# Score products of 64 partitions issued for two heads in turn in both mixers, and four head buffers in the second

## The reference, cut to what matters

```
z = q @ k.T / sqrt(64)                      # per head, over the causal prefix
log_not_b = where(causal, log_sigmoid(-z), 0)
stick = reverse_cumsum(log_not_b) - log_not_b
a = where(causal, exp(log_sigmoid(z) + stick), 0)
out = a @ v

# retention, per head (width 128, rotary applied to q and k)
inner = (q @ k.T * decay) @ v
```

## Time and profile before

| | |
|---|---|
| median of 3 runs | 2847.84 us (2845.98 to 2852.53) |
| profiled execution | 2845.72 us, its span 2843.9 us |
| TensorE busy | 2767.0 us, 97% of the span |
| VectorE busy | 2099.9 us, 74% |
| ScalarE busy | 1414.8 us, 50% |
| GpSimd busy | 195.7 us, 7% |
| data read | 527.48 MB, 188 GB/s over the span |

### The profile page before, as it was taken

The page is one execution under the profiler, slowest core; times in us unless marked ns, Lnnn a source line. Parts: engine busy times, 40 slices in busy tenths (PEclk is TensorE's granted clock), DMA queues, the critical chain, the costliest instruction groups (busy, mean ns, idle before and its releaser), DMA issues.

```text
span 2843.9 us, 40048 instructions
## 1 busy us (share of the span) xinstructions
PE 2767.0 (97%) x16458; PEld 2357.3 (83%) x16458; DVE 2099.9 (74%) x3106; ACT 1414.8 (50%) x1646; POOL 195.7 (7%) x172
## 2 busy tenths in 40 slices
PE   8989999999999999999999999999999999999998
PEld 7768888788888788888888888887888888888887
DVE  7877867665553679999879955536699999799655
ACT  4454445554456555554443344484555544443443
POOL 0200002010013001210000000030011200000000
PEclk9999999999999999999999999999999999999999
DMA  8857854555553355554445555633445544455554
GB/s 331 310 182 269 320 185 173 196 178 191 192 199 134 119 179 185 187 189 164 164 166 191 177 193 192 228 125 134 171 168 190 192 165 170 157 193 176 188 195 143
DMA packets 75637, 537.41 MB, mean 189 GB/s; under 512 B 8512, under 2 KB 8896, under 8 KB 12096
## 3 DMA queue, kind: packets, MB, share of 16 engines
q1 hardware_dynamic: 75456, 534.86, 53.9%
HBM read 527.48 MB, written 7.34 MB: 188 GB/s over the span
## 4 chain that ended last, share of the span: by engine, by line
PE 65%; issue 22%; DVE 7%; ACT 4%; DMA 2%; POOL 0%; SPq 0%; DVEq 0%; POOLq 0%; ACTq 0%
PE banks L442 18%; PE banks L450 9%; PE banks L516 7%; PE banks L519 7%; PE banks L527 7%; DVE wlo L1480 3%; PE banks L490 2%; ACT whi L999 2%; PE banks L492 2%; PE banks L501 2%; PE banks L464 2%; PE banks L466 2%; PE banks L474 1%; DMA raw<-in_wkv 1%; PE banks L944 1%
## 5 line engine op out<-in xcount | busy, mean ns | idle before, releaser
L999 ACT ACTIVATE whi<-raw 128x2048 fp32r<-128x2048 f32 x438 | 838.9, 1916 | 972.5 <-issue 813.8
L1480 DVE TENSOR_TENSOR wlo<-raw,whi 128x2048 fp32r<-128x2048 f32 x438 | 1006.8, 2299 | 312.5 <-ACT whi L999 297.3
L442 PE MATMUL banks<-ht,whi 128*128 128x512 f32 x2880 | 704.8, 394 | 8.5 <-DVE big L1554 2.8
L442 PEld LDWEIGHTS banks<-ht,whi 128*128 128x128 f32 x2880 | 527.6, 189 | 113.2 <-issue 6.6
L516 PE MATMUL banks<-whi,ht 128*128 128x512 f32 x1152 | 458.1, 398 | 13.5 <-DVE ht L1544 9.0
L519 PE MATMUL banks<-whi,ht 128*128 128x512 f32 x1152 | 452.7, 393 | 0.0
L450 PEld LDWEIGHTS banks<-ht,wlo 128*128 128x128 f32 x2880 | 369.1, 191 | 14.6
L450 PE MATMUL banks<-ht,wlo 128*128 128x256 f32 x2880 | 373.4, 282 | 0.0
L527 PE MATMUL banks<-wlo,ht 128*128 128x512 f32 x1152 | 290.6, 390 | 0.0
L516 PEld LDWEIGHTS banks<-whi,ht 128*128 128x128 f32 x1152 | 217.7, 189 | 58.9 <-issue 14.6
L519 PEld LDWEIGHTS banks<-whi,ht 128*128 128x128 f32 x1152 | 217.7, 189 | 43.2
(11 more groups left out here) (274 smaller groups left out, 3425.0 us busy)
## 6 DMA issues: line engine op xcount, KB each, us to landing
raw<-in_pu SPq DMA_DIRECT2D x128, 1024.0 KB, 4.9
raw<-in_pv SPq DMA_DIRECT2D x128, 1024.0 KB, 4.9
raw<-in_win SPq DMA_DIRECT2D x52, 1024.0 KB, 5.0
big<-in_wmod SPq DMA_DIRECT2D x24, 1024.0 KB, 6.6
raw<-in_wmod SPq DMA_DIRECT2D x24, 1024.0 KB, 5.0
raw<-in_wgate SPq DMA_DIRECT2D x22, 1024.0 KB, 4.9
raw<-in_wup SPq DMA_DIRECT2D x22, 1024.0 KB, 5.2
raw<-in_wdown SPq DMA_DIRECT2D x22, 1024.0 KB, 4.9
```

Of the source, the lines that this page charges most:

```text
L442: m = e.matmul(bank[b + n], h[:, q, c[n]], M.both[:, q * 512:(q + 1) * 512], start=q == 0, stop=False, skip_group_check=True)
L999: e.activation(whi(j), slot[u][0], ACT.Copy).then_inc(*hi.mark(j))
L1480: e.tensor_tensor(wlo(j), slot[u][0], whi(j).bitcast(F32), ALU.subtract).then_inc(*lo.mark(j))
```

## The change

In the first mixer the one-head scores of steps 0 to 7 are issued two heads at a time in steps 0, 2, 4 and 6. In the second mixer the logits of two heads are issued in turn behind units 2, 4, 6 and 8, the two heads' `sticks` behind units 3, 5, 7 and 9, and the values behind units 5, 7, 9 and 10. ScalarE, VectorE and GpSimd follow that order, the ring has four buffers, and GpSimd's rotary steps 0 and 2 stand behind the logits' masks of steps 6 and 8, while 1 and 3 stand ahead of the exponentials' masks of steps 7 and 9. Retention's scores are issued for two heads in turn.

```diff
--- before.py
+++ after.py
@@ -661,7 +661,8 @@
 
             def step(i):
                 if i < 8:
-                    scores(0, (i,))
+                    if i % 2 == 0:
+                        scores(0, (i, i + 1))
                 elif i < 12:
                     scores(2, (2 * (i - 8), 2 * (i - 8) + 1))
                 if l == 0 and i == 13:
@@ -739,19 +740,23 @@
                 on.wait_ge(*normal.at((*name, "diag")))
                 e.matmul(bank[b][:, 0:256], ONES, DG[0], start=True, stop=True).then_inc(*turned.mark(("rows", l)))
 
-            def logits(h):
-                b = clear(("sb", l, h), 2 + h % 2)
-                on.wait_ge(*took_v.at(("f", l, 2 * (h // 4) + 1)))
-                p0, c = 64 * (h % 2), h // 2
+            def logits(c):
+                for h in (2 * c, 2 * c + 1):
+                    clear(("sb", l, h), 2 + h % 2)
+                on.wait_ge(*took_v.at(("f", l, 2 * (c // 2) + 1)))
                 for i in range(3):
-                    q = AG[p0:p0 + 64, SBQ + c * 256 + (i > 0) * 128:][:, 0:128]
-                    k = AG[p0:p0 + 64, SBK + c * 256 + (i > 1) * 128:][:, 0:128]
-                    m = e.matmul(bank[b][:, i * 128:(i + 1) * 128], k, q, start=i == 0, stop=True, skip_group_check=True)
-                m.then_inc(*scored.mark(("sb", l, h)))
+                    for h in (2 * c, 2 * c + 1):
+                        p0 = 64 * (h % 2)
+                        q = AG[p0:p0 + 64, SBQ + c * 256 + (i > 0) * 128:][:, 0:128]
+                        k = AG[p0:p0 + 64, SBK + c * 256 + (i > 1) * 128:][:, 0:128]
+                        m = e.matmul(bank[2 + h % 2][:, i * 128:(i + 1) * 128], k, q, start=i == 0, stop=True,
+                                     skip_group_check=True)
+                        if i == 2:
+                            m.then_inc(*scored.mark(("sb", l, h)))
 
             def sticks(h):
                 b = 2 + h % 2
-                s = ag(RING + (h % 3) * 768 + 384, 384)
+                s = ag(RING + (h % 4) * 768 + 384, 384)
                 tneg, oneg = ag(TN, 128), ag(TN + 128, 128)
                 on.wait_ge(*p_keep.at(("soft", l, h)))
                 on.wait_ge(*d_k2.at(l))
@@ -768,25 +773,28 @@
                     clear(("ov", l, 1), 1)
                 on.wait_ge(*p_keep.at(("exp", l, h)))
                 on.wait_ge(*took_a.at(("sv", l, 1)))
-                w = ag(RING + (h % 3) * 768, 384)
+                w = ag(RING + (h % 4) * 768, 384)
                 o = slice(h * 64, h * 64 + 64)
                 v = [ag(SBV + t * 512 + h * 64, 64) for t in range(2)]
                 e.matmul(bank[0][:, o], w[:, 0:128], v[0], start=True, stop=True)
                 e.matmul(bank[1][:, o], w[:, 128:256], v[0], start=True, stop=False)
                 e.matmul(bank[1][:, o], w[:, 256:384], v[1], start=False, stop=True).then_inc(*valued.mark(("sb", l, h)))
 
-            def retention_scores(h):
-                b = clear(("ret", l, h))
+            def retention_scores(c):
+                of = [bank[clear(("ret", l, 2 * c + j))] for j in range(2)]
                 on.wait_ge(*p_mul.at(("r", l, 3)))
-                p0, c = 64 * (h % 2), h // 2
-                q = [AG[p0:p0 + 64, RQ + c * 512 + i * 256:][:, 0:256] for i in range(2)]
-                k = [AG[p0:p0 + 64, RK + c * 512 + i * 256:][:, 0:256] for i in range(2)]
+                q, k = ([[AG[64 * j:64 * j + 64, x + c * 512 + i * 256:][:, 0:256] for i in range(2)] for j in range(2)]
+                        for x in (RQ, RK))
                 for i in range(2):
-                    e.matmul(bank[b][:, 0:256], k[i][:, 0:128], q[i], start=i == 0, stop=i == 1, skip_group_check=True)
+                    for j in range(2):
+                        e.matmul(of[j][:, 0:256], k[j][i][:, 0:128], q[j][i], start=i == 0, stop=i == 1,
+                                 skip_group_check=True)
                 for i in range(2):
-                    m = e.matmul(bank[b][:, 256:384], k[i][:, 128:256], q[i][:, 128:256], start=i == 0, stop=i == 1,
-                                 skip_group_check=True)
-                m.then_inc(*scored.mark(("ret", l, h)))
+                    for j in range(2):
+                        m = e.matmul(of[j][:, 256:384], k[j][i][:, 128:256], q[j][i][:, 128:256], start=i == 0,
+                                     stop=i == 1, skip_group_check=True)
+                        if i == 1:
+                            m.then_inc(*scored.mark(("ret", l, 2 * c + j)))
 
             def retention_values(h):
                 if h == 0:
@@ -814,21 +822,19 @@
                     b_unit([("rv", l, t) for t in range(2)], HT, i - 10, ready)
                 else:
                     b_unit([("rg", l, t) for t in range(2)], HT, i - 12, ready)
-                if 5 <= i < 12:
-                    for h in {5: (0, 1)}.get(i, (i - 4,)):
-                        stick_values(h)
-                if 3 <= i < 11:
+                for h in {5: (0, 1), 7: (2, 3), 9: (4, 5), 10: (6, 7)}.get(i, ()):
+                    stick_values(h)
+                if i in (3, 5, 7, 9):
                     sticks(i - 3)
-                if 2 <= i < 10:
-                    logits(i - 2)
+                    sticks(i - 2)
+                if i in (2, 4, 6, 8):
+                    logits(i // 2 - 1)
                 if i == 11:
                     retention_scores(0)
-                    retention_scores(1)
                 if i == 12:
                     retention_values(0)
                     retention_values(1)
-                    retention_scores(2)
-                    retention_scores(3)
+                    retention_scores(1)
                 if i == 13:
                     retention_values(2)
                     retention_values(3)
@@ -1244,10 +1250,10 @@
 
             def logits(h):
                 key = ("sb", l, h)
-                w = ag(RING + (h % 3) * 768, 384)
+                w = ag(RING + (h % 4) * 768, 384)
                 on.wait_ge(*scored.at(key))
-                if h >= 3:
-                    on.wait_ge(*valued.at(("sb", l, h - 3)))
+                if h >= 4:
+                    on.wait_ge(*valued.at(("sb", l, h - 4)))
                 since()
                 e.activation(w, psum(key)[:, 0:384], ACT.Abs).then_inc(*a_soft.mark((*key, 0)))
                 on.wait_ge(*a_soft.at((*key, 0)))
@@ -1258,7 +1264,7 @@
             def sticks(h):
                 key = ("sb", l, h)
                 on.wait_ge(*scored.at(("stick", l, h)))
-                e.activation(ag(RING + (h % 3) * 768, 384), psum(key)[:, 0:384], ACT.Exp).then_inc(*took_a.mark(key))
+                e.activation(ag(RING + (h % 4) * 768, 384), psum(key)[:, 0:384], ACT.Exp).then_inc(*took_a.mark(key))
 
             os = [ag(OO2 + t * 1024, 1024) for t in range(2)]
             sqs = [XN2[:, 512:1024], XN2[:, 1024:1536]]
@@ -1283,10 +1289,12 @@
                         on.wait_ge(*inv.at(name))
                         e.activation(ag(to + t * 512, 512), psum(key)[:, :], func, scale=RMS[:, t:t + 1]).then_inc(
                             *took_a.mark(key))
-                if 3 <= i < 11:
+                if i in (3, 5, 7, 9):
                     sticks(i - 3)
-                if 2 <= i < 10:
+                    sticks(i - 2)
+                if i in (2, 4, 6, 8):
                     logits(i - 2)
+                    logits(i - 1)
                 if i == 11:
                     for t in range(2):
                         key = ("ov", l, t)
@@ -1848,13 +1856,12 @@
                 if 1 <= i < 4:
                     for j in (0, 1) if i == 1 else (i,):
                         first(j)
-                if 2 <= i < 10:
-                    h = i - 2
+                for h in (i - 2, i - 1) if i in (2, 4, 6, 8) else ():
                     key = ("sb", l, h)
-                    w = ag(RING + (h % 3) * 768, 768)
+                    w = ag(RING + (h % 4) * 768, 768)
                     on.wait_ge(*a_soft.at((*key, 2)))
-                    if h >= 3:
-                        on.wait_ge(*valued.at(("sb", l, h - 3)))
+                    if h >= 4:
+                        on.wait_ge(*valued.at(("sb", l, h - 4)))
                     since()
                     e.scalar_tensor_tensor(w[:, 384:768], psum(key)[:, 0:384], 0.0, w[:, 0:384], ALU.max,
                                            ALU.add).then_inc(*took_v.mark(key))
@@ -2353,16 +2360,16 @@
                 e.tensor_tensor(pair(table), pair(table), ROWS, ALU.mult).then_inc(*p_mul.mark(("tables", l)))
             on.wait_ge(*p_mul.at(("tables", l)))
             for i in range(14):
-                if 6 <= i < 10:
+                if i in (7, 9):
                     rotary(i - 6)
-                if 3 <= i < 11:
-                    h = i - 3
+                for h in (i - 3, i - 2) if i in (3, 5, 7, 9) else ():
                     on.wait_ge(*took_a.at(("sb", l, h)))
-                    keep(ag(RING + (h % 3) * 768, 384), ("exp", l, h))
```

(8 more changed lines are left out.)

## The result

The changed kernel takes 2875.93 us (median, 2872.14 to 2876.68), the kernel before 2847.90 us in the same rounds: 1.0093 times as long, 95% interval 1.0076 to 1.0111. It is slower, as forecast, but by 28.0 us instead of 15.2, and above the upper end of the range (2869 us).

What follows compares the result with a forecast made beforehand. TensorE's own pace was taken to bound the kernel nearly everywhere. Second mixers +6.8 (waits less savings) and +9.6 (slow clock), first mixers +0.6 and -1.8, made +15.2 us: median 2863 us, range 2850 to 2869 us.

Steps and rivals of the forecast that it cites:

- side-by-side products: TensorE's scores, logits and retention for two heads in turn: savings of 5.5, 6.9 and 3.9 us, 16.3 us together.
- The third rival: Logits: side-by-side work fails, a pair costs 1.72 us, time 2865 us; chance 0.06.
- (a): Second mixer, step 3: TensorE waits 2.7 us for head 1's sticks, where before it waited for nothing.
- (b): Second mixer, step 5: TensorE waits 4.5 us at head 0's values for ScalarE's scaled `sv`, 3.2 more than before.
- (c): Second mixer, steps 7 and 9: TensorE waits about 0.3 us each for the second head's sticks.
- the drain of 1.38 us a load: ScalarE, by the skill page, behind each table load; it would make this part's waits each 2.8 us longer.
- (d): Second mixer, step 10: TensorE waits 2.3 us for heads 6 and 7's masks, behind GpSimd's rotary steps.
- the clock: Second mixers: TensorE's clock falls behind waits over 2 us, some 1.6 us each, 9.6 us in all.
- First mixers: Paired scores: layer 0 loses 0.6 us, slow clock behind step 8's wait included; layer 1 gains 1.8 us.
- The clock holds: Rival: the waits come as counted but TensorE's clock doesn't fall, +4.0 us, 2852 us; chance 0.15.
- the logits fail: Rival: two heads' logits don't run side by side, a pair costs 1.72 us, 2865 us; chance 0.06.
- The pairing pays: Rival, second mixer steps 3 to 10: ScalarE's block for a pair is short, 11.9 us saved, 2836 us; chance 0.09.

Runs made afterwards that it cites:

- e8: The changed kernel with the logits' matmuls made head after head, three and three, instead of in turn: 2876.14 us, 1.0085 times the kernel before.
- e4: e1 with ScalarE working a pair off as Abs, Abs, Exp, Exp, Ln, Ln: 2839.68 us, 0.9964 times the kernel before.
- e5: The changed kernel with ScalarE's order Abs, Abs, Exp, Exp, Ln, Ln, GpSimd's masks not moved: 2852.89 us, 1.0002 times the kernel before.
- e7: The changed kernel with VectorE's low-part subtraction cut from 2048 to 64 columns in units 7 to 12 of each second mixer: 2862.45 us, 1.0040.
- e1: The changed kernel with GpSimd's exponentials' masks ahead of the rotary steps in steps 7 and 9 of the second mixer: 2861.90 us, 1.0037.
- e6: The changed kernel with 5, 9 and 15 unread products for TensorE in the second mixer's three waits: 2871.54 us, 1.0076 times the kernel before.
- e2: The kernel before with only the first mixer's scores paired, in steps 0, 2, 4 and 6: 2845.29 us, 0.9982 times the kernel before.
- e10: e4 with the first mixer's scores of layer 0 made one head at a time: 2845.04 us, 0.9976 times the kernel before.
- e11: e4 run again, unchanged, in the same rounds as e10: 2841.20 us, 0.9967 times the kernel before.

## Why the prediction was right and wrong

**Right: the side-by-side products.** Scores, logits and retention came at 1.09 (176.12 to 177.21 us), 0.87 and 1.52 us a pair; forecast were 1.09, 0.86 and 1.5. The third rival fell; that two heads in a row would need 1.72 us was wrong too (1.2 us from start to start in e8).

**Right: (a) and (b).** 2.6 and 4.5 us against 2.7 and 4.5 forecast, by ScalarE's order as it was worked out. e4 and e5 remove most of both by taking out one pair of table loads. (c), forecast at 0.6 us a layer, isn't there. The 2.8 us that the prediction named beside the drain of 1.38 us a load were miscounted, as four loads stand ahead of (a), 5.5 us; nothing hangs on it, for the trace shows no drain: the load of 835.55 is over at 836.83, and Exp starts at 836.84.

**Wrong: (d), the step that failed.** "Their masks stand on GpSimd behind rotary steps 2 and 3, 893.30 - 889.07 = 4.23 us each": the price came from a step that ran beside a split only for its first 0.4 us, and was carried to a place where three splits run. It measured 14.1 us for two, and the wait 7.8 us instead of 2.3, 5.5 us a layer. This is shown from both sides, by e7 (the splits cut to 64 columns, the wait 1.7 us) and e1 (the masks out from behind, the wait 1.8 us). The second mixers' waits grew by 2.6 + 3.1 + 7.8 = 13.5 us a layer, not 8.8, which is 9.4 of the 15.8 us that the sum was short. With this step right the time would have fallen into the range (2875.9 - 11 = 2865 us); e7 is 0.40% slower than the kernel before, and 0.53% was forecast.

**Undersized: the clock.** Subtracting 13.5 - 5.4 = 8.1 us from 13.4 and 14.5 leaves 5.3 and 6.4 us a layer, 11.7 in all, where 9.6 stood. In layer 0 it cost nothing at (a), 2.45 us at (b) by e6, and some 2.8 us at (d), half of the 5.6 us from 912.9 to 918.5 at the lower level: 5.25 us. In layer 1 the clock fell behind (a) too: from the second head's sticks to the next logits TensorE took 1878.90 - 1870.77 = 8.13 us instead of 850.93 - 844.37 = 6.56 us, 1.6 us more. One price of 1.6 us for every wait over 2 us came true there alone: it came from waits of 2.0 and 2.7 us and was used for 4.5 us and more. That the whole was off by only 2.1 us is luck, since 0 at one wait stood against 2.45 and 2.8 at others. And e6 shows that such a sum is not what filling the waits gives back.

**First mixers.** Layer 1 is right (-1.4 for -1.8; e2 -1.5). Layer 0 came out 1.4 us above its term. The nine kernels with paired scores there had stages of 63.7 to 68.2 us (mean 65.9), the four with single scores 62.9 to 64.4 (mean 63.4), and the medians of e10 and e11 say the opposite. The slow clock that the term counted behind the wait of step 8 is there in the changed kernel and not in e2. What a pair does in that stage stays open below some 2 us, and so do the 2.5 us ahead of the first scores, which moved between 131.8 and 136.3 us in kernels that are the same up to there.

**The rivals.** "The clock holds" and "the logits fail" are out by the rows above. "The pairing pays" named its place rightly, ScalarE's block for a pair: e4 took it to 5.28 us in step 2 and 3.85 us in step 4, where the rival asked for 3.7, and with the masks moved that was enough for 2839.7 us.

## What to carry to other kernels

Two heads at a time saves an engine's time only as far as the engines behind it can take two at a time: order their work by function (one table load for both heads), and put what the fast engine waits for ahead of what nobody waits for yet. The duration of a GpSimd product or mask held here only beside the VectorE work it was measured with, so when a change moves GpSimd work, lay both timelines over each other first. A lengthened wait on TensorE can cost more than itself, through the clock: 0 to 2.8 us a wait here.

## What the runs showed of the hardware that was not expected

- GpSimd's tensor products and masks, and VectorE's subtraction of two tensors in SBUF, hold each other up: a product of 0.73 or 1.29 us takes 2.8 or 3.35 us beside a split, a pair of masks 2.82 instead of 0.77 us, a split 2.98 instead of 2.29 us; with the splits cut short all are back.
- Two heads' three logits matmuls on opposite halves of the partitions take 1.26 us head after head and 0.94 us in turn, not 1.7 against 0.9.
- The same wait of 2.60 us was followed by a clock of 1.00 in layer 0 and 0.74 in layer 1, one of 2.70 us by 1.00 (e2) and of 2.71 us by 0.59 (changed kernel), one of 2.25 us by 0.61 (e8), and one of 1.47 us by 1.00 in e4 and of 1.48 us by 0.73 in e11, which are the same kernel. The length of one wait alone does not decide it.
